# First turn of the block inverses on VectorE, and smaller unread products on TensorE, in a two-block transformer kernel

## The reference

```python
a_mat = jnp.where(tri_strict, beta[..., None] * kk * decay, 0.0)
...
a_full = jnp.broadcast_to(a_mat + eye, (b, h, n, c, c))
sol = lax.linalg.triangular_solve(a_full, rhs, left_side=True, lower=True,
                                  unit_diagonal=True)
```

## Time and profile before

| | us |
|---|---|
| median of 3 runs | 905.58 |
| lowest and highest | 905.33, 905.67 |
| the profiled execution | 904.91 |
| its span, first to last instruction | 903.2 |

### The profile page before, as it was taken

The page is one execution under the profiler, slowest core; times in us unless marked ns, Lnnn a source line. Parts: engine busy times, 40 slices in busy tenths (PEclk is TensorE's granted clock), DMA queues, the critical chain, the costliest instruction groups (busy, mean ns, idle before and its releaser), DMA issues.

```text
span 903.2 us, 15634 instructions
## 1 busy us (share of the span) xinstructions
PE 892.1 (99%) x6451; PEld 826.8 (92%) x6451; DVE 572.7 (63%) x824; ACT 498.2 (55%) x771; POOL 136.0 (15%) x151
## 2 busy tenths in 40 slices
PE   8999999999999999999999999999999999999998
PEld 8999999889999988788899989999999899998886
DVE  4556554878888745666767796865467655554542
ACT  5576864556565634557775754333454565554330
POOL 6011101611111100133344110000100011110000
PEclk9999999999999999999999999999999999999999
DMA  8843264675655557347444545442346556656550
GB/s 276 280 151 118 94 233 152 222 219 180 202 197 165 189 209 236 129 151 263 156 149 158 161 139 167 133 141 70 102 144 199 187 159 204 198 187 199 184 200 23
DMA packets 132595, 156.33 MB, mean 173 GB/s; under 512 B 9354, under 2 KB 106029, under 8 KB 132269
## 3 DMA queue, kind: packets, MB, share of 16 engines
q1 hardware_dynamic: 125844, 151.78, 51.6%
q10 hardware_dynamic: 6680, 3.56, 1.3%
HBM read 153.08 MB, written 2.24 MB: 172 GB/s over the span
## 4 chain that ended last, share of the span: by engine, by line
PE 88%; DVE 6%; ACT 3%; issue 1%; DMA 1%; POOL 1%; SPq 0%; POOLq 0%; ACTq 0%
PE ps L1969 75%; PE ps L1924 4%; PE ps L2000 3%; PE ps L2224 2%; PE ps L1921 2%; DVE wl L825 1%; DVE gkq L859 1%; DVE gv L859 1%; DMA raw<-in_w_in 1%; PE ps L2195 1%; DVE mt L1258 1%; ACT wh L1417 1%; ACT gkq L1622 0%; ACT sS L1608 0%; PE ps L2107 0%
## 5 line engine op out<-in xcount | busy, mean ns | idle before, releaser
L825 DVE TENSOR_TENSOR wl<-raw,wh 128x1024 fp32r<-128x1024 f32 (+1 forms) x275 | 326.6, 1205 | 187.1 <-ACT wh L1417 186.9
L1969 PE MATMUL ps<-xh,wh 128*128 128x256 f32 x1280 | 357.9, 283 | 0.6 <-ACT xh L1465 0.4
L1969 PE MATMUL ps<-xh,wl 128*128 128x256 f32 x1280 | 350.4, 277 | 0.0
L1969 PE MATMUL ps<-xl,wh 128*128 128x256 f32 x1280 | 348.2, 277 | 0.0
L1417 ACT ACTIVATE wh<-raw 128x1024 fp32r<-128x1024 f32 (+1 forms) x292 | 286.6, 1024 | 110.7 <-PE ps L1969 88.8
L1969 PEld LDWEIGHTS ps<-xh,wh 128*128 128x128 f32 x1280 | 239.0, 188 | 3.9 <-issue 1.7
L1969 PEld LDWEIGHTS ps<-xh,wl 128*128 128x128 f32 x1280 | 238.7, 188 | 0.0
L1969 PEld LDWEIGHTS ps<-xl,wh 128*128 128x128 f32 x1280 | 238.0, 188 | 0.3
L666 POOL TENSOR_TENSOR wl<-raw,wh 128x1024 fp32r<-128x1024 f32 (+1 forms) x17 | 44.3, 2603 | 81.7 <-ACT wh L1417 81.4
L1969 PE MATMUL ps<-wh,f2L 128*128 128x512 f32 x128 | 49.8, 389 | 0.0
L1969 PE MATMUL ps<-wh,f2H 128*128 128x512 f32 x128 | 49.8, 389 | 0.0
(11 more groups left out here) (324 smaller groups left out, 1383.7 us busy)
## 6 DMA issues: line engine op xcount, KB each, us to landing
raw<-in_w_in SPq DMA_DIRECT2D x55, 1024.0 KB, 5.0
raw<-in_w_up SPq DMA_DIRECT2D x38, 1024.0 KB, 5.1
raw<-in_w_down SPq DMA_DIRECT2D x26, 1024.0 KB, 5.0
raw<-in_w_out SPq DMA_DIRECT2D x8, 1024.0 KB, 5.0
raw<-in_w_proj_fox SPq DMA_DIRECT2D x4, 1024.0 KB, 5.2
raw<-in_w_proj_gdn SPq DMA_DIRECT2D x4, 1024.0 KB, 5.0
raw<-in_w_conv_branch SPq DMA_DIRECT2D x4, 512.0 KB, 3.4
raw<-in_w_att_branch SPq DMA_DIRECT2D x4, 512.0 KB, 3.3
```

The lines of the kernel that those rows point to most:

```text
L825: e.tensor_tensor(L, R, H.bitcast(F32), ALU.subtract).then_inc(lo.sem)
L1969: k = e.matmul(o, l, r, start=opens, stop=done and n == ends[c], skip_group_check=True)
```

## The change

1. At level 0 TensorE no longer transposes `Yt`. DVE copies `Y16` with its two inner axes exchanged into a new tile `Z16`; both go to DRAM and come back as `Zc` and `Yc`; DVE spreads `Zc` into `Tm` (four instructions, chains 0 to 3) and `Yc` into `Yt` (four instructions, each two ticks behind). ACT's copy of level 0 is gone.
2. `level_at` and `solve_at` are two ticks earlier, so the first product of level 0 stands at tick 75, where the transpose stood, and the second at tick 78 instead of 80. `o_turn` starts two ticks earlier too.
3. `settle` moves 16 columns instead of 128, to the last columns of its bank; only the one in `rest_of_gains` keeps 128. `settle` is added at the end of `norm` (executed twice) and after the products `C` in `attention` of s = 1 (executed four times).
4. In the second half of the norm between the blocks, the low part of unit `U_FQ + 2`, half 1, is made ahead of `x2_scaled(1)` on DVE.

```diff
 def level_at(c, i):
-    return 75 + 2 * c + 8 * i
+    return 73 + 2 * c + 8 * i
 def solve_at(g):
-    return 106 + 2 * g
+    return 104 + 2 * g
...
-                for c in range(4):
+                e.wait_ge(*b16("s", 14))
+                copy(Z16[:], Y16[:].rearrange("p i j -> p j i")).then_inc(b16t.sem)
+
+                def spread(dst, src, c):
                     a, g = c // 2, c % 2
+                    e.tensor_tensor(dst[:, a, 4 * g:4 * g + 4, :].rearrange("p h (n j) -> p h n j", j=16),
+                                    src[:, 8 * a + 4 * g:8 * a + 4 * g + 4, :].unsqueeze(2).broadcast_to([P, 4, 8, 16]),
+                                    mid(M16[:], 4).rearrange("p h (n j) -> p h n j", j=16), ALU.mult).then_inc(ch_start[c].sem)
+
+                e.wait_ge(*cst("m2"))
+                for c in range(6):
                     yield from at.to(START_Y + c)
-                    e.wait_ge(inverses_in, 16)
...
+                    if c < 4:
+                        e.wait_ge(turned_in, 16)
+                        spread(Tm, Zc, c)
+                    if c >= 2:
+                        e.wait_ge(inverses_in, 16)
+                        spread(Yt, Yc, c - 2)
...
             low(U_FQ + 2, 0)
+            low(U_FQ + 2, 1)
             x2_scaled(1)
-            low(U_FQ + 2, 1)
...
-                e.wait_ge(*b16("s", 14))
-                e.dma_start(inverses[:], Y16[:].rearrange("p i j -> p (i j)")).then_inc(inverses_out, 16)
+                e.wait_ge(*b16t("t"))
+                for k, src in enumerate((Z16, Y16)):
+                    e.dma_start(inverses[k], src[:].rearrange("p i j -> p (i j)")).then_inc(inverses_out, 16)
                 yield from at.to(INVERSES_IN)
-                e.wait_ge(inverses_out, 16)
-                e.dma_start(Yc[:], inverses[:].rearrange("p x -> (p x)").rearrange("(a s j) -> s a j", s=P, j=16)
-                            ).then_inc(inverses_in, 16)
+                e.wait_ge(inverses_out, 32)
+                for k, (dst, landed) in enumerate(((Zc, turned_in), (Yc, inverses_in))):
+                    e.dma_start(dst[:], inverses[k].rearrange("p x -> (p x)").rearrange("(a s j) -> s a j", s=P, j=16)
+                                ).then_inc(landed, 16)
...
-            def settle(bank):
-                mul(PS[bank][:, 0:P], ident[0:64, :], ident[0:64, :])
+            def settle(bank, n=16, rows=slice(0, 64)):
+                mul(PS[bank][:, 512 - n:512], ident[rows, :], ident[rows, 0:n])
 # at the end of norm(n):
+                settle(7)
 # in rest_of_gains:
-                settle(6)
+                settle(6, P)
 # in attention(s), behind the products C:
+                    if s:
+                        settle(5, rows=rows)
...
                 for i in levels:
-                    yield from at.to(level_at(c, i))
                     if i:
+                        yield from at.to(level_at(c, i))
                         e.wait_ge(*dv(f"Y{i - 1}"))
+                        for j in range(4):
+                            k = turn(o[j], Y[j])
+                        k.then_inc(me.sem)
+                    yield from at.to(level_at(c, i) + 2)
+                    if i:
+                        e.wait_ge(*ac(f"T{i}"))
                     else:
                         e.wait_ge(*dv("rv"))
-                        e.wait_ge(*ch_start[c]("Y"))
-                    for j in range(4):
-                        k = turn(o[j], Y[j])
-                    k.then_inc(me.sem)
-                    yield from at.to(level_at(c, i) + 2)
-                    e.wait_ge(*ac(f"T{i}"))
+                        e.wait_ge(*ch_start[c]("Z"))
                     products(AT, Z)
                     yield from at.to(level_at(c, i) + 5)
                     e.wait_ge(*dv(f"U{i}"))
+                    if i == 0:
+                        e.wait_ge(*ch_start[c]("Y"))
                     products(Z, Y)
```

More of the change, by code:

```diff
@@ L236, in two_blocks @@
         Yc = reg("Yc", [P, 16, 16], 51)
+        Z16 = reg("Z16", [P, 16, 16], 52)
+        Zc = reg("Zc", [P, 16, 16], 53)
         blocks = nc.dram_tensor("blocks", [16, P + 1, P], F32)
-        inverses = nc.dram_tensor("inverses", [P, 256], F32)
+        inverses = nc.dram_tensor("inverses", [2, P, 256], F32)
         gz = reg("gz", [P, 8, T], 60)
@@ L372, in two_blocks @@
         gat = steps("gdn_decayed", "x", "y")
-        blocks_out, blocks_in, inverses_out, inverses_in = (
-            sem(n) for n in ("blocks_out", "blocks_in", "inverses_out", "inverses_in"))
+        blocks_out, blocks_in, inverses_out, inverses_in, turned_in = (
+            sem(n) for n in ("blocks_out", "blocks_in", "inverses_out", "inverses_in", "turned_in"))
         b16p = steps("blocks_start", "z", "i")
         b16 = steps("blocks_inverse", "m", "s")
+        b16t = steps("blocks_turned", "t")
         levels = range(len(LEVELS))
-        ch_pe = [steps(f"chain_pe{i}", "tv", *(f"{k}{i}" for i in levels for k in ("t", "p", "y"))) for i in range(4)]
-        ch_act = [steps(f"chain_act{i}", *(f"T{i}" for i in levels)) for i in range(4)]
+        ch_pe = [steps(f"chain_pe{i}", "tv", *(f"{k}{i}" for i in levels for k in ("t", "p", "y") if i or k != "t")) for i in range(4)]
+        ch_act = [steps(f"chain_act{i}", *(f"T{i}" for i in levels[1:])) for i in range(4)]
         ch_dve = [steps(f"chain_dve{i}", "rv", *(f"{k}{i}" for i in levels for k in ("U", "Y"))) for i in range(4)]
-        ch_start = [steps(f"chain_start{i}", "Y") for i in range(4)]
+        ch_start = [steps(f"chain_start{i}", "Z", "Y") for i in range(4)]
         so_pe = [steps(f"solve_pe{i}", "W0", "Z", "o0", "W1", "o1") for i in range(2)]
@@ L1127, in gdn @@
                         yield from at.to(INVERT + (m + 1) // 2)
-                for c in range(4):
+                e.wait_ge(*b16("s", 14))
+                copy(Z16[:], Y16[:].rearrange("p i j -> p j i")).then_inc(b16t.sem)
+                def spread(dst, src, c):
                     a, g = c // 2, c % 2
-                    yield from at.to(START_Y + c)
-                    e.wait_ge(inverses_in, 16)
[L1132 to L1135, removed]
+                    e.tensor_tensor(dst[:, a, 4 * g:4 * g + 4, :].rearrange("p h (n j) -> p h n j", j=16),
[3 more added lines that the diff above has]
+                for c in range(6):
+                    yield from at.to(START_Y + c)
+                    if c < 4:
[4 more added lines that the diff above has]
+                        spread(Yt, Yc, c - 2)
             def turned_v(c):
@@ L1344, in vector @@
             for i in range(4):
-                unit(U_G2 + i, 5 if i == 1 else None, lambda: side.add(o_turn()))
+                unit(U_G2 + i, 3 if i == 1 else None, lambda: side.add(o_turn()))
             for i in range(4):
@@ L1668, in chain @@
                 at = Ticks()
-                for i in levels:
+                for i in levels[1:]:
                     yield from at.to(level_at(c, i) + 1)
@@ L2354, in tensor @@
             for u in range(U_GZ, U_YG):
-                unit(u, XH, XL, at=5 if u == U_G2 + 1 else None, begins=lambda: side.add(o_turn()))
+                unit(u, XH, XL, at=3 if u == U_G2 + 1 else None, begins=lambda: side.add(o_turn()))
             for i in range(4):
```

## The result

The changed kernel takes 910.19 us in the median of six runs (907.76 to 911.68), the kernel before on the same chip 905.52. A seventh run took 1815.56 us, twice as long at full clock, for a cause that nothing here shows; it is left out (with it the median is 910.84). The ratio of the means is 1.0049, 95% interval 1.0037 to 1.0060: slower by half a per cent, where 0.8% was forecast. The profiled execution took 909.54 us, with a span of 907.8 against 903.2. The forecast for that execution was +7.2; it is +4.6.

What follows compares the result with a forecast made beforehand. TensorE's own work was taken as the bound (88% of the last-ending chain). Terms -0.86 + 2.4 + 0 - 0.8 + 3.8 + 2.7 = +7.2 on 904.91 gave 912.1, plus 0.67 for the median: 912.8 us, range 904.6 to 916.5.

Steps and rivals of the forecast that it cites:

- Smaller settles, -0.86: Eleven settles shrink to 16 columns, nine of them gaining about 0.095 us from the second product's streaming: -0.86 us (0 to -1.6).
- Added settles in the attention, +2.4: Four settles behind products C cost 0.515 us each, +2.06; with changes of pace behind them +2.4 us (1.2 to 3.9).
- Both terms on the pace: First attention: stretches behind C keep the quick pace, -0.53 us; the long stretch from 114 us may turn slow, +0.9.
- Norms, 0: Settles ending the two norms: +0.14 us, then -0.45 from a quicker stretch; about +0.3 at the second; sum about 0.
- The moved low part, -0.8: Norm between the blocks: with `wl` made before `xs` on DVE, TensorE's 1.38 us distance becomes 0.32: -0.8 us (0 to -1.2).
- it fills that gap: Norm between the blocks: `wl`, made first, fills DVE's 0.72 us idle time before `xs`, which starts 0.4 us late.
- The inverses' stretch, +3.8: Level 0: TensorE waits 5 us for DVE's mask of chain 0; +2.8, two ticks +1.4, transpose -0.44: +3.8 us (+2.0 to +6.5).
- `Zc` lands 5.9 us later: Inverses' way through DRAM: read-back issued at 577.2, landing 5.9 us later, so DVE starts to spread at 583.1.
- The clock, +2.7: Behind the 5 us wait TensorE's clock falls from 2.4 to 1.2 GHz, losing +2.7 us (0 to +3).
- the wait without the clock: Rival, 20%: the wait ahead of `Yt,Tm` is shorter than 5 us or the clock level stays: 910.1 us.
- The paces turn against it: Rival, 10%: 16-column settles leave TensorE in the slow pace, 4.7 and 3.4 us behind `U_UP` and `U_UP2`: about 917 us.
- Side savings carry it: Rival, 12%: the read-back lets spreading start by 577.5 or spreads are quick; the inverses' stretch gives -1.75: 902.2 us.

Runs made afterwards that it cites:

- the last kernels: Changed kernel six ticks later, without added settles, the four `Yc` spreads behind their chains' masks: 902.86 us; the same with the `rest_of_gains` settle at 16 columns: 903.15 us.

## Why the prediction was right

The side was right, and so were the wait for DVE's mask and the clock behind it; the time lay in the range. What starts the spreading, and the sum as one of terms that add up, were not. By its steps:

- **Smaller settles, -0.86.** 0.093 us each was measured for 0.095, and -0.83 in all. Where it goes was named wrongly: the first of the two products gave 0.08 (from 0.213 to 0.133) and the second 0.013, not the other way round.
- **Added settles in the attention, +2.4.** They cost 0.50 each, +2.0 in sum up to the inverses, forecast +2.06. In the time of the whole kernel they were not seen: without them the wait and the clock took the 2 us. The sum added them in full to a wait that takes up what TensorE saves ahead of it. Both terms on the pace came to nothing. The stretches behind C stayed slow in the same three rounds: 40 products now fit from 54.9 to 59.6, where 42 did, with the first 0.45 us taken by the settle. The long stretch stayed quick. The two terms (-0.53 and +0.9) erred in opposite ways, so the sum was near by luck.
- **Norms, 0.** The settle of the first norm costs 0.13, the second one's some 0.2. The first stretch turned quick (-0.43), and the stretch from 23 to 45 turned slow (+0.39). Neither hangs on that settle. With the same code at the place, the first stretch was quick in five traces and slow in two; without the settle it was quick in three and slow in three.
- **The moved low part, -0.8.** -0.33 in the trace (its own two numbers, 1.06 less 0.37, give 0.7). The step that failed is "it fills that gap": the 0.72 us in which DVE stood idle was GpSimd's time for the power, and DVE's work in it lengthened the power from 0.55 to 1.41. Counted from the first low part, `xs` starts 3.93 us behind it and 3.07 with the low part put back, and TensorE waits 0.66 for it. The Trainium skill, "SBUF — State Buffer", section "SBUF: two separate sides", says that VectorE and GpSimd share a port pair that a VectorE instruction with two SBUF inputs holds to its end against a GpSimd instruction that reads SBUF. The traces agree: the low part reads `raw` and `wh`, the power ends 0.4 us behind it. So this low part could not fill the idle 0.72 us without lengthening the power.
- **The inverses' stretch, +3.8.** Right in what waits for what from the start of the spreading on, in the 8.8 us of DVE's queue and in the two ticks (+1.36) and the transpose (-0.44). The mis-sized term is the start of the spreading, on top of TensorE's lag of 2.0 at that place: 582.72 was measured where 583.1 plus the lag would be 585.1. The read-back of `U16` landed in 5.8 us in place of 7.1, which let `Y16` be ready only 0.6 us later (573.55 against 572.95), and the way from there to the first spread took 9.2 us, not 10.15. The step that failed is "`Zc` lands 5.9 us later": it landed after 4.7 us, and the spreading did not wait for it but for a low part behind ACT's queue, which the issue of the second read-back held for 3.25 us. The prediction gave that issue no price. That 582.72 lies so near 583.1 is luck. So the stretch cost 2.38 - 2.03 + 1.36 - 0.44 = 1.3 us and not 3.8, and the wait was 3.4 us and not 5. This was one execution: with the low part put back the same way took 10.8 us and the wait 4.6, near the forecast.
- **The clock, +2.7.** It fell, to the level foreseen, for 3.4 us: 1.7 us lost. In three of six runs of the changed kernel the mean clock is 0.996, as in the execution above that spent 6.8 us at half, worked for 5.66 of them and so lost 2.8. These three take 910.84 to 911.68; at 0.998 to 1.00 it is 907.76 to 909.54. So by their mean clock half of the runs lost about what was forecast, and the profiled one less. By the Trainium skill, "TensorE: Matmul & The Clock Gate", section "What's actually happening", throttled is the default and activity releases it. The fall behind 3.4 us without work agrees with it.

Of the rivals, *the wait without the clock* (910.1) lies nearest by number, on the median itself, and the wait was shorter than 5 us as it says; but the clock did fall. *The paces turn against it* is refuted by the smaller settles alone. *Side savings carry it* is what the last kernels did, once the mask came early enough: 902.86 against the 902.2 that the rival gave, though without the settles in the attention, which it counted with +1.2.

**What stays open.** Why the way through memory takes 8.7 us in one execution and 11.1 in another was not settled. What differs is the landing of the second transfer out, 6.4 and 6.3 us behind its issue in the two long ones and 2.4 to 4.5 in the others. In all of them a weight load of 1 MB is issued 0.8 us behind the second transfer out. Issuing that transfer took 1.7 and 1.95 us where the way was long (11.1 and 10.8), and 0.5 to 1.2 in the others. No run changed the time of the weight load. Open, too, is what sets TensorE's pace of 0.113 or 0.118 us behind a side product.

## What to carry to other kernels

A transfer through memory in place of work on the bounding engine saves that work only while its way has cover, and the cover has to hold the longest way, not the one of the trace: here a wait turned savings of 1.7 us into a loss of 4.7, and a kernel that waited 1.7 us in its profiled run took 1.5 to 4.4 us longer in six of ten runs. Look in the trace for what comes last at the end of the way: here it was not the landing but the queue of the engine that issued the transfers. Look on the waited-for engine for work that is not needed yet: four spreads moved behind the masks gave 3.7 us. And work saved ahead of a wait comes back as a longer wait, so take the wait away first and measure the savings then.

## What the runs showed of the hardware

- TensorE's granted clock halved (1.2 GHz) behind 3.4 us without work, for 3.4 us. Behind 4.6 us without work it was half for 6.8 us in one execution and for 3.4 in another. It stayed full behind 1.7 and 2.0 us in the profiled runs.
- A GpSimd instruction of 128 elements took 1.41 us beside a VectorE instruction that reads two SBUF tiles, 0.55 with VectorE idle; another took 0.99 beside such an instruction and 0.19 beside one that reads a PSUM and an SBUF tile.
- A 64-row product of 128 columns takes TensorE 0.21 us as the first of two and 0.20 as the second; with 16 columns it is 0.13 and 0.19.
- The issue of a DMA of 128 KB on ACT's queue took 0.34 to 0.38 us when it was the first of two, and 0.5 to 3.3 us as the second, when an equal one stood in front of it. ACT's next weight part waited for it, and through it VectorE's.
- The pace of 256-column products at full clock behind the same code was 0.113 us in one build's trace and 0.118 in another's.
